# Modulation products with the weights moving in four column groups, interleaved column pieces and a finer first wait in the second block

## The reference, cut to what matters

```python
silu_c = jax.nn.silu(c)                # (1, 1024)
silu_cc = jax.nn.silu(c_ctx)           # (1024,)
for l in range(DEPTH):
    mx = jnp.split((silu_c @ w_mod[l] + b_mod[l])[:, None, :], N_MOD, axis=-1)
    mc = jnp.split(silu_cc @ w_mod[l] + b_mod[l], N_MOD, axis=-1)
    zx = modulate(rms_norm_2(x, norm1_g[l]), mx[0], mx[1]) @ w_in[l]
    zc = modulate(rms_norm_2(ctx, norm1_g[l]), mc[0], mc[1]) @ w_in[l]
    ...
    x = x + mx[2] * mixer_rest(fx, gx, attn_x, l)      # ends in concatenate([y_f, attn, y_c]) @ w_o
    hx = modulate(rms_norm_2(x, norm2_g[l]), mx[3], mx[4])
    x = x + mx[5] * channel_mlp(hx, l)
```

## Time and profile before

| | |
|---|---|
| median of 3 runs | 4130.52 us (4129.41 to 4133.31) |
| the profiled execution | 4130.38 us |
| its span, first to last instruction | 4128.6 us |
| PE busy | 3891.5 us (94%) |
| DVE busy, ACT busy | 1744.0 us, 1534.1 us |
| granted TensorE clock, mean | 0.955 |
| chain that ended last | PE 85%, DVE 7%, ACT 3%, DMA 3%, issue 2% |

### The profile page before, as it was taken

One profiled execution on the slowest core, in us unless ns is written; L12 is line 12 of the kernel. 1 busy time (PEld: TensorE's weight loads), 2 busy tenths in 40 slices (PEclk: granted clock), 3 DMA queues, 4 the chain that ended last, 5 costly groups with the idle time before them and its releaser, 6 DMA issues.

```text
span 4128.6 us, 45135 instructions
## 1 busy us (share of the span) xinstructions
PE 3891.5 (94%) x16959; PEld 2860.4 (69%) x16959; DVE 1744.0 (42%) x2372; ACT 1534.1 (37%) x2269; POOL 2.4 (0%) x9
## 2 busy tenths in 40 slices
PE   7999899999999998999999799988999989989998
PEld 5666678788876665787788574457888876447886
DVE  4565443433355664434333434523222244434333
ACT  4454332333334544323333334423223224433333
POOL 0000000000000000000000000000000000000000
PEclk8999999999999999999999799988999989999999
DMA  4222233233332222333333210001222222002332
GB/s 126 82 81 83 72 92 94 84 92 92 96 97 77 83 76 77 92 95 90 87 94 94 87 51 21 0 26 46 61 62 65 61 64 71 1 20 83 92 92 81
DMA packets 570351, 303.37 MB, mean 73 GB/s; under 512 B 26017, under 2 KB 564977, under 8 KB 570225
## 3 DMA queue, kind: packets, MB, share of 16 engines
q1 hardware_dynamic: 568496, 299.32, 25.1%
q10 hardware_dynamic: 1728, 2.36, 0.2%
HBM read 299.55 MB, written 2.10 MB: 73 GB/s over the span
## 4 chain that ended last, share of the span: by engine, by line
PE 85%; DVE 7%; ACT 3%; DMA 3%; issue 2%; SPq 0%; DVEq 0%; ACTq 0%
PE ps L959 12%; PE ps L960 12%; PE ps L961 12%; PE ps L1134 9%; PE ps L1136 9%; PE ps L1135 9%; PE ps L1304 2%; DMA wraw<-in_w_mod 2%; PE ps L1287 2%; PE ps L1263 2%; PE ps L1077 2%; PE ps L1013 1%; PE ps L1046 1%; PE ps L1011 1%; PE ps L1058 1%
## 5 line engine op out<-in xcount | busy, mean ns | idle before, releaser
L1402 ACT ACTIVATE whi<-wraw 128x1024 fp32r<-128x1024 f32 x544 | 572.1, 1053 | 722.9 <-DMA wraw<-in_w_mlp 256.2
L1859 DVE TENSOR_TENSOR wlo<-wraw,whi 128x1024 fp32r<-128x1024 f32 x544 | 665.1, 1223 | 343.4 <-ACT whi L1402 327.9
L959 PE MATMUL ps<-uhi,whi 128*128 128x512 f32 x1440 | 640.1, 445 | 20.8 <-DVE ulo L1876 20.7
L960 PE MATMUL ps<-ulo,whi 128*128 128x512 f32 x1440 | 582.7, 405 | 0.0
L961 PE MATMUL ps<-uhi,wlo 128*128 128x512 f32 x1440 | 582.2, 404 | 0.0
L1134 PE MATMUL ps<-u2hi,whi 128*128 128x512 f32 (+1 forms) x1024 | 379.0, 370 | 34.2 <-DVE u2lo L2102 32.1
L959 PEld LDWEIGHTS ps<-uhi,whi 128*128 128x128 f32 x1440 | 279.3, 194 | 157.7 <-issue 78.0
L1135 PE MATMUL ps<-u2lo,whi 128*128 128x512 f32 (+1 forms) x1024 | 372.9, 364 | 0.0
L1136 PE MATMUL ps<-u2hi,wlo 128*128 128x512 f32 (+1 forms) x1024 | 372.7, 364 | 0.0
L1134 PE MATMUL ps<-yhi,whi 128*128 128x512 f32 x960 | 345.2, 360 | 5.8 <-DVE ylo L2208 5.8
L1135 PE MATMUL ps<-ylo,whi 128*128 128x512 f32 x960 | 345.0, 359 | 0.0
(11 more groups left out here) (250 smaller groups left out, 5090.8 us busy)
## 6 DMA issues: line engine op xcount, KB each, us to landing
wraw<-in_w_in SPq DMA_DIRECT2D x128, 512.0 KB, 3.9
wraw<-in_w_mlp SPq DMA_DIRECT2D x128, 512.0 KB, 3.9
wraw<-in_w_mod SPq DMA_DIRECT2D x96, 512.0 KB, 4.0
wraw<-in_w_mlp_in SPq DMA_DIRECT2D x64, 512.0 KB, 4.1
wraw<-in_w_mlp_out SPq DMA_DIRECT2D x64, 512.0 KB, 3.8
wraw<-in_w_branch SPq DMA_DIRECT2D x16, 512.0 KB, 3.4
wraw<-in_w_out SPq DMA_DIRECT2D x16, 512.0 KB, 3.8
wraw<-in_w_o SPq DMA_DIRECT2D x16, 512.0 KB, 3.8
```

Source lines behind the costliest of these rows:

```text
L959: pe.matmul(bank, whs[:, i], x_hi[:, k], start=(i == 0), stop=False)
L960: pe.matmul(bank, whs[:, i], x_lo[:, k], start=False, stop=False)
L1402: act.activation(whi[:, r], wraw[:, r], ACT.Copy).then_inc(w_hi, 1)
L1859: dve.tensor_tensor(wlo[:, r], wraw[:, r], whi[:, r].bitcast(F32), ALU.subtract).then_inc(w_split, 1)
```

## The change

**Modulation.** `silu_parts` becomes the stationary operand in plain float32, 32 columns wide (two values, 30 zeros), and the raw weights move, 128 columns at a time. The eight pieces go to four column groups of the array, so to four groups of 32 PSUM partitions, two pieces in each. ACT and DVE no longer round and split these chunks (`plan.whole`; `parted` recounts the semaphores). The result stands as rows, so new steps turn it: DVE copies each chunk's 128 x 128 result to `mod_rows` (`mod_kept`), PE transposes four at a time (`mod_turn`) and DVE adds (`mod_summed`). The chunks are spread over 31 slots instead of 34: the first three have none, 14 have one and 17 have two, the second of which stands half a place later.

**Wide chunks.** The loop over column pieces goes inside that over the eight row pieces.

**`w_o`.** The waits ahead of its first chunk become waits of the pieces: piece 5 for the attention output, 6 and 7 for the two tiles of the convolution. PE also drops a wait for `turned_free` in `mla_turned`.

```diff
@@ head_schedule
-    for i, end in enumerate(ends):
-        for c in range(MOD_COLS * i // len(ends), MOD_COLS * (i + 1) // len(ends)):
-            put(end - 0.9, "mod", layer=layer, column=c)
+    late = ends[HI_AHEAD:]
+    for i, end in enumerate(late):
+        mods = range(MOD_COLS * i // len(late), MOD_COLS * (i + 1) // len(late))
+        for c in mods:
+            at = end - (0.9 if c in mods[:1] else 0.45)
+            made = put(at, "mod", layer=layer, column=c)
+            put(at + 0.2, "mod_kept", head=made)
+            if c % MOD_GROUP == MOD_GROUP - 1:
+                turn = put(at + 0.4, "mod_turn", head=made)
+                put(at + 0.7, "mod_summed", head=turn, layer=layer, column=c - MOD_GROUP + 1)
@@ PE, first block
                     elif step.name == "mod":
-                        pe.wait_ge(w_split, step.chunk + 1)
+                        r = step.chunk % RAW
+                        pe.wait_ge(raw_in[r], 16 * (step.chunk // RAW) + 16)
                         pe.wait_ge(silu_ready, 1)
                         bank_wait(pe, bank_evac, step.tile)
-                        for k in range(KT):
-                            pe.matmul(ps[:, step.tile % 2, 0:4], whs[:, k], silu_parts[:, k, :], start=(k == 0),
-                                      stop=False)
-                            last = pe.matmul(ps[:, step.tile % 2, 0:4], wls[:, k], silu_parts[:, k, :],
-                                             start=False, stop=(k == KT - 1))
+                        for half in range(2):
+                            for group in range(4):
+                                rows, k = slice(32 * group, 32 * (group + 1)), 4 * half + group
+                                last = pe.matmul(ps[rows, step.tile % 2, 0:P], silu_parts[:, k, :], raw[:, k],
+                                                 start=(half == 0), stop=(half == 1))
                         last.then_inc(chunk_done, 1)
+                    elif step.name == "mod_turn":
+                        for tile in step.kept:
+                            bank_done(pe, bank_evac, tile)
+                        bank_wait(pe, aux_free, step.aux)
+                        for c in range(MOD_GROUP):
+                            last = pe.transpose(ps[:, AUX + step.aux % 2, P * c:P * (c + 1)],
+                                                mod_rows[:, P * c:P * (c + 1)], ident[:, :])
+                        last.then_inc(mod_turned, 1)
@@ wide_chunk_product
-                for lo, hi in pieces(width):
-                    for k in range(KT):
-                        if split is not None and lo == 0:
-                            pe.wait_ge(lo_ready, split + k + 1)
...
+                for k in range(KT):
+                    if split is not None:
+                        pe.wait_ge(lo_ready, split + k + 1)
+                    if ready is not None and k in ready:
+                        pe.wait_ge(*ready[k])
+                    for lo, hi in pieces(width):
                         pe.matmul(out[:, lo:hi], whs[:, k], x_hi[:, k, lo:hi], start=(k == 0), stop=False)
+                    for lo, hi in pieces(width):
                         pe.matmul(out[:, lo:hi], whs[:, k], x_lo[:, k, lo:hi], start=False, stop=False)
+                    for lo, hi in pieces(width):
                         last = pe.matmul(out[:, lo:hi], wls[:, k], x_hi[:, k, lo:hi], start=False, stop=(k == KT - 1))
@@ PE, mla_turned; ahead of w_o
-                        bank_wait(pe, turned_free, step.turned)
...
-                for b in range(2):
-                    bank_done(pe, bank_evac, s.mixed_tiles - 2 + b)
-                pe.wait_ge(mla_att_free, s.mixed_outs)
+                made = {5: (mla_att_free, s.mixed_outs)}
+                for t in range(2):
+                    n = s.marks["conv_map", t]
+                    made[6 + t] = (bank_evac[n % 2], n // 2 + 1)
@@ ACT: hi_after (DVE: lo_before likewise)
-                if chunk + HI_AHEAD < plan.chunks:
+                if chunk + HI_AHEAD < plan.chunks and chunk + HI_AHEAD not in plan.whole:
                     weight_hi(chunk + HI_AHEAD)
@@ DVE, first block
                     elif step.name == "mod":
                         lo_before(step.chunk)
-                        dve.wait_ge(chunk_done, step.chunk + 1)
-                        dve.tensor_reduce(mod[:, step.layer, step.column, :],
-                                          ps[:, step.tile % 2, 0:4].rearrange("p (s v) -> p v s", v=2), axis=AX.X,
-                                          op=ALU.add).then_inc(bank_evac[step.tile % 2], 1)
+                    elif step.name == "mod_kept":
+                        made = step.head
+                        dve.wait_ge(chunk_done, made.chunk + 1)
+                        if step.summed:
+                            dve.wait_ge(mod_turned, step.summed)
+                        at = P * (made.column % MOD_GROUP)
+                        dve.tensor_copy(mod_rows[:, at:at + P], ps[:, made.tile % 2, 0:P])\
+                            .then_inc(bank_evac[made.tile % 2], 1)
+                    elif step.name == "mod_summed":
+                        dve.wait_ge(mod_turned, step.sum + 1)
+                        ...
```

More of the change, by code:

```diff
@@ L81 @@
 UNIT_START, UNIT_SPACE = 18, 2.85
+MOD_GROUP = 4
 BRANCH_TILES = {"diff": (0, 1, 2, 3), "ret": (11, 8, 9, 10), "gqa": (4, 5, 6, 7)}
@@ L226, in number_steps @@
             s.chunk, s.tile = num["chunk"](), num["tile"]()
+        elif name == "mod_kept":
+            s.summed = last.get("mod_turns", 0)
+            last.setdefault("kept", []).append(s.head.tile)
+        elif name == "mod_turn":
+            s.aux, s.kept = num["aux"](), last.pop("kept")
+            last["mod_turns"] = last.get("mod_turns", 0) + 1
+        elif name == "mod_summed":
+            s.sum = num["mod_sum"]()
         elif name == "head_norm":
@@ L410, in number_mixer @@
             s.y = num["y"]()
+            if s.name == "conv_map":
+                mark[s.name, s.t] = s.tile
         elif s.name == "key_rotate":
@@ L464, in __init__ @@
         num = self.num = {k: Seq() for k in (
-            "max head chunk tile rope sq value swish aux root normed rot turn decay unit pair w attend final_sq "
+            "mod_sum max head chunk tile rope sq value swish aux root normed rot turn decay unit pair w attend final_sq "
             "conv_in conv_done conv_normed ring y key_rope mla_rope mla_peak mla_log mla_row mla_turned mla_att mla_out mid "
@@ L475, in __init__ @@
             s.heads_split_end = num["split"].n
+            self.whole += [step.chunk for step in s.heads if step.name == "mod"]
             s.out = self.linear(KT)
@@ L503, in __init__, with parted @@
         assert self.chunks % RAW == 0
+    def parted(self, chunk):
+        return chunk - sum(c < chunk for c in self.whole)
     def norm(self, tiles, bank="aux", width=SEQ):
@@ L995, in _ @@
                         if i == 0:
-                            pe.wait_ge(w_split, whole.chunk + 1)
+                            pe.wait_ge(w_split, plan.parted(whole.chunk) + 1)
                             bank_wait(pe, bank_evac, whole.tile)
@@ L1090, in _ @@
                     elif step.name == "branch":
-                        pe.wait_ge(w_split, step.chunk + 1)
+                        pe.wait_ge(w_split, plan.parted(step.chunk) + 1)
                         pe.wait_ge(att_free if step.n == 2 else lo_ready, step.ready)
@@ L1342, in _ @@
                         chunk, tile = s.out.chunk + b, s.out.tile + b
-                        pe.wait_ge(w_split, RAW * i + (chunk + 1))
+                        pe.wait_ge(w_split, RAW * i + (plan.parted(chunk) + 1))
                         pe.wait_ge(bank_evac[tile % 2], RAW // 2 * i + tile // 2)
-                        wide_chunk_product(ring(tile), chunk % RAW, yhi, ylo, s.width).then_inc(chunk_done, 1)
+                        wide_chunk_product(ring(tile), chunk % RAW, yhi, ylo, s.width,
+                                           ready=None if b else made).then_inc(chunk_done, 1)
                 wide_norm(s.norm2)
@@ L1419, in sigmoid @@
                 return act.activation(*operands, ACT.Sigmoid, **more)
-            for chunk in range(HI_AHEAD):
-                weight_hi(chunk)
+            for chunk in range(-HI_AHEAD, 0):
+                hi_after(chunk)
             def root_of(n_root, aux, count, eps, use):
@@ L1861, in lo_before @@
             def lo_before(chunk):
-                if chunk + LO_AHEAD < plan.chunks:
+                if chunk + LO_AHEAD < plan.chunks and chunk + LO_AHEAD not in plan.whole:
                     weight_lo(chunk + LO_AHEAD)
-            for chunk in range(LO_AHEAD):
-                weight_lo(chunk)
+            for chunk in range(-LO_AHEAD, 0):
+                lo_before(chunk)
             def inverse_root(n_root):
```

33 lines of the change are left out of this document (15 added, 18 removed).

## The result

The changed kernel takes **4005.5 us** (median of four runs, 4002.5 to 4008.6) against 4131.3 us: a ratio of 0.9695, 95% interval 0.9679 to 0.9712, 126 us less. The forecast was 4022 us, within 3980 to 4076. The time came out 16 us under the forecast. Of all executions told of here one, the fourth of `mod_alone`, was slow (9630 us) and is in no median.

What follows compares the result with a forecast made beforehand. PE, busy 94% of the span, was taken to bound the kernel. From 4130.4 us, slots -40, clock -54, added idle +8, wide chunks -13 and `w_o` -9 gave 4022 us; the 8-in-10 range was 3980 to 4076.

Steps and rivals of the forecast that it cites:

- The chunk, 0.85 us: One modulation chunk on PE: 1.70 us before, 0.85 after, with 0.4 for going to column groups and back; bounds 0.65 and 2.1.
- The slots, -40: Modulation slots of both layers: shorter chunks save 20 us a layer, 40 in all, limited by waits.
- The floor: Two-chunk slots: the next projection waits for `whi`, `wlo` and the added DVE copy, at least 3.3 to 3.8 us.
- The clock, -54 and +8 back: Two modulation stages: 70% of 77 us lost to half clock returns, 54 us; 8 us booked for PE idle growing.
- The factor 0.45: Share of half-clock time counted as lost, from full-width matmuls 0.24 us apart at full clock and 0.43 at half.
- Both are off the path, and I book nothing: DVE and ACT lose 48 `wlo` and 48 `whi` a layer; claimed off the path, booked at nothing.
- Wide chunks, -13, bounds 8 and 16: First chunk behind each of three wide norms: 4.3 us less each, 13 us in all, bounds 8 and 16.
- w_o, -9: Ahead of `w_o`: two waits, 5.8 us, go and an estimated 3 us of half clock; 9 us, bounds 5 and 11.
- 0, with bounds of 5 us: Wide chunks where nothing waits: reordering the same matmuls gains 0, bounds 5 us either way, for 28 chunks.
- More comes back: Rival, 17%: all clock falls go, relieved DVE and ACT answer sooner, chunk at 0.65 us; 3983 us.
- The turns cost more: Rival, 10%: each of 24 modulation turns holds PE for 2 us because DVE's copy is late; 4070 us.
- Slower: the groups one after another: Rival, 5%: column groups don't overlap, chunk 2.1 us, clock no better; 4160 us, deciding from about 1.55 us a chunk.

Runs made afterwards that it cites:

- mod_alone: The changed kernel with the wide-chunk loop order, the waits ahead of `w_o` and the `turned_free` wait as before, so only the modulation edit is left: 4036.9 us.
- fuller_thin: The kernel before with each of a modulation chunk's 16 matmuls moving 128 columns (the four, 32 times over) instead of four: 4111.5 us, ratio 0.9955.
- one_group: The changed kernel with all eight pieces of a modulation chunk in one column group instead of two in each of four: 4033.6 us, ratio 0.9759.
- hi_early: The changed kernel with ACT making `whi` in front of its wait for a projection chunk, not behind its emptying: 4005.3 us, ratio 0.9693.
- turn_late: The changed kernel with each `mod_turn` ahead of the next slot's first modulation chunk, and `mod_rows` a ring of six rows: 4004.0 us, ratio 0.9686.
- layout: The kernel before with only the changed kernel's places in SBUF (wider `silu_parts`, unused `mod_rows`): 4118.8 us, ratio 0.9970.
- shift96: The changed kernel with an unused buffer of 96 bytes per partition behind `silu_parts`: 4006.8 us, ratio 0.9700.

## Why the prediction held, point by point

- **PE bounds the kernel, and a thin matmul costs by the clock.** Right in its mechanism: `fuller_thin` raises the clock to 0.96 with the loads, waits and order of the program left as they were, and no run contradicts it. That every microsecond off PE comes off the time was wrong for the modulation stages. There 124 us of PE's work (`one_group`) was worth 28.
- **The chunk, 0.85 us.** It takes 0.57, and 0.66 with the passage ahead of it, which the 0.85 took in. The passes are as forecast (16 / 4 x 0.107 = 0.43, or 0.46 at the 0.116 that `one_group` measured); the passage, put at 0.4, is about 0.2: 0.11 in the 0.57 and 0.09 in the gap of 0.32 ahead. By the earlier trace rows it should have been 0.4, so the attend's passage is no measure for this one. The Trainium skill's page TensorE: Matmul & The Clock Gate, section Wait — 56ns, not 53.3ns?, gives the 62 ns of the prediction, an estimated 1.0 us for a chunk, only for the case that the hardware's decoding is off, and beside it a floor of about 25 ns between starts. Here 16 passes take 0.57 us, 36 ns each: above the second, and the first doesn't bind; which way the matmuls were decoded no run tells. What the Trainium skill's page TensorEngine Tiling, section Key Properties, says of draining at a change of the tiling mode may be in the 0.2; no run separates it.
- **The slots, -40.** The floor is there: in the slot at 136 us `wlo`, the copy and the turn follow one another as told, and `hi_early` with `turn_late` takes 20 us of these waits off a layer. But the floor was priced as the only thing between the slots' work and the time, and removed waits came back, in part, as waits for `probs`. No run prices this term by itself.
- **The clock, -54 and +8 back.** The step that failed most. The clock rose nearly as forecast: of 172 us at half clock after has some 65 left, so 62% went, where the prediction took 70. But in `fuller_thin`, where 53% went with nothing else changed, it is worth 21 us (15 of them in the two stages), not 46: the 92 us at full clock should have given 42, and idle rose by 15 and 10 us in the two stages, not 4. The factor 0.45 gives PE's time, and the kernel's only where PE has no partner with a fixed time; the softmax between `score` and `turn` is one.
- **"Both are off the path, and I book nothing"** for the 48 + 48 rounded and split chunks that ACT and DVE no longer make. This was wrong. `one_group` and `fuller_thin` have chunks of nearly the same length (1.86 and 1.73 us), the same softmax places and the new form's lighter DVE (238 instead of 284 us busy in a stage) and ACT (191 instead of 236), and `one_group`'s stages are 20.1 and 19.3 us shorter. In its first stage PE waits 8.2 us for `probs` (5.3 and 2.9), against 26.1, and its idle is 26 us, against 48. The way from a score's last pass to its `probs` step, 8.9 us in the mean in before and 9.1 in `fuller_thin`, is 7.9 in `one_group` and 7.8 in after (first stage, 48 such steps): the chain itself got shorter when DVE and ACT were relieved. How much of the 39 us is that is only argued: the two kernels also differ in where the chunks and turns stand and in the clock (0.99 and 0.96), which by the prediction's own factor would be worth up to 27 of the 39. By the stages the modulation is 15 for the clock, 39 for the form and 33 for the four groups, 87 in all; by the medians, without the places, it is 82 to 85. The prediction had 86, from 40 + 54 - 8. That it came so near is luck: a sum of parts of the wrong size.
- **Wide chunks, -13, bounds 8 and 16.** Right behind a norm: the first chunk of the second block lasted 2376.28 - 2356.02 = 20.3 us (from its first matmul, the line below, to the next chunk's in the earlier trace rows) and lasts 15.8, as the timeline of after shows (its first piece; the next chunk):

```profile
2356.02 0.77 PE L1134 MATMUL ps<-u2hi,whi 128*128 128x512 f32 x1 [5.45 <-DVE u2lo L2102]
```

```profile
2265.32 0.98 PE L1166 MATMUL ps<-u2hi,whi 128*128 128x512 f32 x2 [5.44 <-DVE u2lo L2142]
...
2281.11 0.51 PE L1166 MATMUL ps<-u2hi,whi 128*128 128x512 f32 x2
```

  2281.11 - 2265.32 = 15.8: 4.5 us less, forecast 4.3. The term that was mis-sized is the order elsewhere, "0, with bounds of 5 us": it is worth about 10, and the count of 28 chunks was wrong too, there are 84. The measured 26 us lies outside all bounds given for this edit (8 to 16, with 5 either way); the 21 us of the trace lie at their edge.
- **w_o, -9.** 8.2 us measured alone, and no wait is left at L1166 for `yhi` (0.0 in the page line of after). Right.
- **The places in SBUF, 12 us.** In no term. The diff did show that `silu_parts` grew, and nothing in the trace of before could have told what that does.
- **The sum.** Forecast -108, from 86 + 13 + 9: measured alone 82 to 85 + 26 + 8 + 12 = 128 to 131, together 126. What was missing is the places (12 us) and the wide chunks (13 us), less 1 to 4 us of the modulation, 1 of `w_o`, and 2 to 5 that are lost where the edits meet; the wide chunks' share of the places, some 4 us by the 67.20 of `layout` against 67.58, is such a loss.
- **The rivals.** *More comes back* named 3983 and was nearest on the chunk, but not all falls of the clock went. *The turns cost more* was half right: PE waits 2.0 us for each of ten turns a layer, but `turn_late`, which leaves 5.3 of the 19.7 us in the first stage, gains 1.5 us. *Slower: the groups one after another*, deciding from 1.55 us a chunk, falls: `one_group` has 1.86 and is 98 us faster than before. It had left the clock as it was; in `one_group` it is 0.99.
- **The signs.** The two stages were to last about 460 us at 0.97, and last 466 and 462 at 0.96 and 0.97; idle was to stay under 70, and is 60 and 58. The waits were to be for `wlo`; they are for the copy behind it.

## What to carry to other kernels

Where the busiest engine runs in step with a chain of fixed length on others, here `score`, softmax, `turn`, a microsecond taken off it was worth between a fifth and somewhat over a third of itself here: 124 us of matmuls were worth 28, and the 42 us of clock in `fuller_thin` 15 in its stages. Moving the turns by a fifth to three fifths of a place was worth 25 with no work removed. After any edit that shortens an engine's work between two such steps, read the waits for the chain again and set the distances anew. And before a small difference is put down to an edit, look at a stretch that it doesn't touch: if its spacing moved too, it is the places of the buffers.

## What the runs showed that was not expected

- The spacing of full-width matmuls hangs on where the buffers lie in SBUF: 234.3, 233.3 and 232.4 ns in three sets of places, and 66.56 or 67.42 us for eight wide chunks. 896 bytes are worth 12 us in this kernel.
- Moving two column pieces for each product in turn (512, 256, 512, 256) is 1.5% quicker than all 512-column pieces and then all 256-column ones: 66.56 against 67.58 us for 384 matmuls, with no wait in either. It hangs on the places too: 66.56 against 67.20 in those of after, and 67.42 in those of `shift96`.
- Work taken off DVE and ACT, 42% and 37% busy, shortened the way from score to `probs` from 8.9 to 7.8 us.
- The clock can be held up by useless work: 128 instead of 4 columns in the thin matmuls leave their length nearly as it was (1.73 instead of 1.70 us a chunk) and lift the granted clock of the stage from 0.91 to 0.96.
